# A value projection in seven block products instead of eight, on one Trainium2 core

## What is computed

```
xn = rms_norm(h, norm_in_g)
proj = einsum('btd,de->bte', xn, w_in)              # 1024 x 6144
q, k, v, g_ret, x_lru, g_lru = split(proj, 6)       # 1024 columns each
q = rotary(q); k = rotary(k) * 128 ** -0.5
scores = einsum(q, k) * decay_mat                   # 8 heads of 128, causal, decays by head
o_ret = group_norm_heads(scores @ v);  y_ret = o_ret * silu(g_ret)
xc = causal_depthwise_conv(x_lru)
o_lru = rg_lru(xc, gates);             y_lru = o_lru * silu(g_lru)
h = h + concat(y_ret, y_lru) @ w_out
```

## Time and profile before

| | |
|---|---|
| median of 3 runs | 2059.18 us (2058.5 to 2060.09) |
| the profiled execution: device time | 2056.59 us |
| its span | 2054.8 us |
| TensorE busy | 98% of the span |
| VectorE, GpSimd, ScalarE busy | 55%, 49%, 18% |
| mean granted TensorE clock | 0.996 |

### The profile page before, as it was taken

The page is one execution under the profiler, slowest core; times in us unless marked ns, Lnnn a source line. Parts: engine busy times, 40 slices in busy tenths (PEclk is TensorE's granted clock), DMA queues, the critical chain, the costliest instruction groups (busy, mean ns, idle before and its releaser), DMA issues.

```text
span 2054.8 us, 39352 instructions
## 1 busy us (share of the span) xinstructions
PE 2020.2 (98%) x16934; PEld 1900.2 (92%) x16934; DVE 1124.1 (55%) x1958; ACT 375.3 (18%) x777; POOL 1015.3 (49%) x775
## 2 busy tenths in 40 slices
PE   8999999999999999999899999999999999999998
PEld 7888887899998999978788999999999999999998
DVE  3535134456515675335757577726772455576752
ACT  1343012133201000024321210001000231120000
POOL 0000000258852788400001568885888677547884
PEclk9999999999999999999999999999999999999999
DMA  8634443344443454523102344444444544434441
GB/s 331 172 126 154 144 164 115 129 165 175 168 165 124 171 175 167 190 103 106 40 5 103 107 160 167 175 172 157 171 165 166 204 162 148 150 116 166 172 176 62
DMA packets 43878, 307.63 MB, mean 150 GB/s; under 512 B 5288, under 2 KB 5544, under 8 KB 7744
## 3 DMA queue, kind: packets, MB, share of 16 engines
q1 hardware_dynamic: 40752, 291.78, 39.9%
q0 software_dynamic: 2096, 7.31, 1.4%
q10 hardware_dynamic: 864, 6.10, 0.7%
HBM read 302.54 MB, written 2.62 MB: 149 GB/s over the span
## 4 chain that ended last, share of the span: by engine, by line
PE 91%; DVE 6%; issue 1%; ACT 1%; DMA 0%; DVEq 0%; SPq 0%
PE ps L587 57%; PE ps L252 15%; PE ps L311 5%; PE ps L249 3%; PE ps L271 1%; PE ps L286 1%; DVE sb_work L425 1%; PE ps L1658 1%; DVE sb_xn L2562 1%; DVE sb_work L418 1%; PE ps L1683 1%; PE ps L393 0%; DVE sb_h L788 0%; PE ps L2145 0%; PE ps L2292 0%
## 5 line engine op out<-in xcount | busy, mean ns | idle before, releaser
L587 PE MATMUL ps<-sb_work,sb_ring 128*128 128x128 f32 x3968 | 476.2, 275 | 0.3 <-DVE sb_work L1977 0.3
L587 PEld LDWEIGHTS ps<-sb_work,sb_ring 128*128 128x128 f32 x3968 | 459.4, 192 | 1.0 <-issue 0.5
L555 POOL TENSOR_TENSOR sb_table<-sb_ring 128x512 f32<-128x512 f32 x126 | 161.4, 1281 | 369.0 <-PE ps L587 189.8
L587 PE MATMUL ps<-sb_work,sb_table 128*128 128x128 f32 x2256 | 285.4, 275 | 0.0
L587 PEld LDWEIGHTS ps<-sb_work,sb_table 128*128 128x128 f32 x2256 | 268.4, 192 | 0.0
L558 POOL TENSOR_TENSOR sb_ring<-sb_ring 128x512 f32<-128x512 f32 x189 | 260.7, 1379 | 0.0
L557 POOL TENSOR_TENSOR sb_table<-sb_table,sb_ring 128x512 f32<-128x512 f32 x126 | 176.3, 1399 | 9.9
L587 PE MATMUL ps<-sb_xn,sb_ring 128*128 128x128 f32 x1440 | 175.5, 275 | 0.0
L587 PEld LDWEIGHTS ps<-sb_xn,sb_ring 128*128 128x128 f32 x1440 | 168.6, 192 | 0.4
L560 POOL TENSOR_TENSOR sb_table<-sb_ring,sb_table 128x512 f32<-128x512 f32 x126 | 168.4, 1336 | 0.0
L252 PE MATMUL ps<-sb_work,sb_ring 128*128 128x256 f32 x736 | 162.8, 380 | 0.0
(11 more groups left out here) (442 smaller groups left out, 2909.8 us busy)
## 6 DMA issues: line engine op xcount, KB each, us to landing
sb_ring<-stream SPq DMA_DIRECT2D x275, 1024.0 KB, 4.8
sb_table<-decay ACTq DMA_DIRECT2D x1, 1536.0 KB, 21.0
bias_rows<-sb_relg POOLq DMA_DIRECT2D x1, 1536.0 KB, 34.7
sb_con<-consts ACTq DMA_DIRECT2D x1, 1216.0 KB, 9.7
sb_table<-lora POOLq DMA_DIRECT2D x1, 1152.0 KB, 6.0
sb_h<-x SPq DMA_DIRECT2D x2, 512.0 KB, 5.8
sb_ring<-stream SPq DMA_DIRECT2D x2, 512.0 KB, 7.4
sb_work<-gates ACTq DMA_DIRECT2D x1, 1024.0 KB, 14.3
```

Source lines behind the costliest of these rows:

```text
L555: v.tensor_tensor(s[:, 0], a[1][0], a[1][1], ALU.add).then_inc(S["fw_ready"], 1)
L587: ins = mm(fast_bank(c, g, b)[:, i * P:i * P + P], *(sides[::-1] if token_major else sides), start=first and i == 0 and j == 0, stop=last ...
```

## The change

The v stage becomes four seven-product units. `plan()` now gives it no banks of the turn (the later stages keep the same bank numbers modulo four), and the stage comes first in the list of seven-product stages:

```diff
-("b1_v", 4, 0)
+("b1_v", 0, 4)
-FAST_ORDER = ["b2_ffn", "l0_ffn1", ...]
+FAST_ORDER = ["b1_v", "b2_ffn", "l0_ffn1", ...]
+def early_tile(c, z):
+    if z % PREPS:
+        flat = c.table[:, :, :].rearrange("p a b -> p (a b)")[:, 1536 * (z - 1):1536 * z]
+    else:
+        flat = c.work[4][:, :, :].rearrange("p a b -> p (a b)")[:, 0:1536]
+    return flat.rearrange("p (s k n) -> p s k n", s=3, k=4)
+def fast_base(g):
+    return 2 * (g % 2) + (0 if g < FAST_G["b2_ffn"] else 4)
```

TensorE:

```diff
 def lru_gates(n):
     if n == 0:
-        pe.wait_ge(S["decay_loaded"], 32)
+        pe.wait_ge(S["decay_loaded"], 16)
...
 for u in range(4):
-    p_unit(c, pe, n0 + u, q1 + u, c.xn, token_major=True)
+    pe.wait_ge(S["fw_ready"], 4 * u + 4)
+    if u < 2:
+        for q in (2 * u, 2 * u + 1):
+            c.wait_read(pe, PLAN["b1_k"][1] + q)
+    else:
+        pe.wait_ge(S["fast_read"], u - 1)
+    fast_products(c, pe, n0 + u, u, range(4), lambda k, j, t: c.xn[:, 2 * k + j, t * P:t * P + P],
+                  lambda k, m: xt[:, m, k, :], u, True, True,
+                  (lambda: pe.wait_ge(S["b1_spread"], 4)) if u == 0 else None, True)\
+        .then_inc(S[f"unit_done{(n0 + u) % UNITS}"], 1)
     lru_gates(u + 3)
...
 scores(0)
+pe.wait_ge(S["fast_read"], 3)
 gate_unit(0)
 gate_unit(1)
+pe.wait_ge(S["fast_read"], 4)
 outputs(0)
```

VectorE and ScalarE:

```diff
 for u in range(8):
     rotate(u)
     if u >= 5:
         decay(u - 5)
-for n in range(3, 8):
-    decay(n)
+spread_input(c, dve, c.xn, W[3], S["b1_spread"], 0)
+for u in range(4):
+    if u > 1:
+        dve.wait_ge(S["b1_v_kept"], u - 1)
+    fast_sum(c, dve, u, c.t1[:, u % 2, :], lambda: c.wait_done(dve, PLAN["b1_v"][0] + u), ch)
+    decay(u + 3)
+decay(7)
...
-dve.wait_ge(S["decay_loaded"], 32)
+dve.wait_ge(S["decay_loaded"], 48)
```

```diff
 for u in range(4):
-    c.wait_done(act, n0 + u)
-    c.read(nc.scalar.activation(v[:, :, u * 256:u * 256 + 256],
-                                c.bank(q0 + u).rearrange("p (m n) -> p m n", m=2), ACT.Copy), q0 + u)
+    copy_first(c, act, u)
+    if u > 1:
+        c.wait_done(act, PLAN["b1_v"][0] + u - 1)
+        act.dma_start(c.table[:, 4 * u - 8:4 * u - 4, :], c.decay[:, 4 * u - 8:4 * u - 4, :])\
+            .then_inc(S["decay_loaded"], 16)
+    act.wait_ge(S["fast_read"], u + 1)
+    nc.scalar.activation(v[:, :, u * 256:u * 256 + 256].rearrange("p t (i n) -> p i t n", i=2),
+                         c.t1[:, u % 2, :].rearrange("p (i t n) -> p i t n", i=2, t=2), ACT.Copy)\
+        .then_inc(S["b1_v_kept"], 1)
     lru_gates(u + 3)
...
 act.dma_start(c.gates[:, :, :, :], gates).then_inc(S["decay_loaded"], 16)
-act.dma_start(c.table[:, :, :], decay).then_inc(S["decay_loaded"], 16)
```

GpSimd prepares the four v units after the convolution (which is done with its inputs by then) and before it writes the bias rows:

```diff
+pool.wait_ge(S["b1_conv"], 8)
+prepare_weights(c, pool, "b1_v")

 pool.wait_ge(S["b2_bias_read"], 1)
 pool.dma_start(bias_rows...
```

More of the change, by code:

```diff
@@ L35, in plan @@
     fast = ("fast", 2, 3 * FFI - 2)
-    stages = [("b1_xlru", 4, 0), ("b1_q", 4, 0), ("b1_k", 4, 0), ("b1_v", 4, 0), ("b1_gret", 4, 0),
+    stages = [("b1_xlru", 4, 0), ("b1_q", 4, 0), ("b1_k", 4, 0), ("b1_v", 0, 4), ("b1_gret", 4, 0),
               ("b1_glru", 4, 0), ("b1_out", 0, 8),
@@ L493 @@
 FAST = ["b2_ffn", "l0_ffn1", "l0_ffn2", "l1_ffn1", "l1_ffn2"]
-FAST_ORDER = ["b2_ffn", "l0_ffn1", "l0_x", "l0_ffn2", "l1_ffn1", "gm", "l1_x", "l1_ffn2"]
+FAST_ORDER = ["b1_v", "b2_ffn", "l0_ffn1", "l0_x", "l0_ffn2", "l1_ffn1", "gm", "l1_x", "l1_ffn2"]
 PREPS = 3
@@ L502, in fast_counts @@
     for name in FAST_ORDER:
-        if name == "gm":
+        if name == "b1_v":
+            start, units, outs = PLAN[name][0], 4, 4
+        elif name == "gm":
             start, units, outs = PLAN["gm_v"][0], 22, 18
@@ L525, in x_count @@
     return spread_count(2 * i + 2) - 16
+def early_tile(c, z):
[4 more added lines that the diff above has]
+    return flat.rearrange("p (s k n) -> p s k n", s=3, k=4)
 def prep_tile(c, z):
-    tile = (z + 1) % PREPS
+    if z < FAST_Z["b2_ffn"]:
+        return early_tile(c, z)
+    tile = (z - FAST_Z["b2_ffn"] + 1) % PREPS
     if tile < 2:
@@ L560, in prepare_weights @@
         v.tensor_tensor(s[:, 2], a[0][1], s[:, 1], ALU.subtract).then_inc(S["fw_ready"], 1)
+def fast_base(g):
+    return 2 * (g % 2) + (0 if g < FAST_G["b2_ffn"] else 4)
 def fast_bank(c, g, b):
-    return c.ps[:, 4 + 2 * (g % 2) + b, :]
+    return c.ps[:, fast_base(g) + b, :]
 def fast_products(c, pe, n, z, pairs, xs, ts, g, first, last, before_t=None, token_major=False,
@@ L700, in fast_sum @@
     v, S = c.nc.vector, c.S
-    two = c.ps[:, 4 + 2 * (g % 2):6 + 2 * (g % 2), :].rearrange("p b n -> p (b n)")
+    two = c.ps[:, fast_base(g):fast_base(g) + 2, :].rearrange("p b n -> p (b n)")
     dve.wait_ge(S["fast_p1"], g + 1)
@@ L826, in b1_scalar @@
                                     c.bank(q0 + u).rearrange("p (m t) -> p m t", m=2), ACT.Copy), q0 + u)
-    act.wait_ge(S["b1_abs"], 1)
+    act.wait_ge(S["b1_pad"], 2)
     nc.scalar.activation(c.small[:, 8:16], c.small[:, 0:8], ACT.Exp, scale=-1.0).then_inc(S["b1_exp"], 1)
@@ L857, in b1_scalar @@
             lru_gates(u - 5)
-    n0, q0 = PLAN["b1_v"]
     v = W[2][:, :, :].rearrange("p a b -> p (a b)").rearrange("p (m n) -> p m n", m=2)
     for u in range(4):
-        c.wait_done(act, n0 + u)
-        c.read(nc.scalar.activation(v[:, :, u * 256:u * 256 + 256],
-                                    c.bank(q0 + u).rearrange("p (m n) -> p m n", m=2), ACT.Copy), q0 + u)
+        copy_first(c, act, u)
[7 more added lines that the diff above has]
+            .then_inc(S["b1_v_kept"], 1)
         lru_gates(u + 3)
@@ L924, in b1_tensor @@
             lru_gates(u - 5)
-    n0, q1 = PLAN["b1_v"]
+    n0, _ = PLAN["b1_v"]
+    xt = W[3][:, :, :].rearrange("p a b -> p (a b)").rearrange("p (s k t) -> p s k t", s=4, k=4)
     for u in range(4):
-        p_unit(c, pe, n0 + u, q1 + u, c.xn, token_major=True)
+        pe.wait_ge(S["fw_ready"], 4 * u + 4)
[8 more added lines that the diff above has]
+            .then_inc(S[f"unit_done{(n0 + u) % UNITS}"], 1)
         lru_gates(u + 3)
@@ L947, in outputs @@
             pe.wait_ge(S["b1_gate_i"], 8)
-            c.wait_read(pe, q1 + 3)
-            c.wait_read(pe, q1 + 2)
+            pe.wait_ge(S["b1_v_kept"], 4)
         else:
@@ L1016, in b1_vector @@
     ch.step(v.tensor_scalar(s[:, 16:24], c.p("lru_lambda", 0, 8), -1.0, None, ALU.mult))
-    v.tensor_tensor(s[:, 0:8], s[:, 16:24], c.p("lru_lambda", 0, 8), ALU.max).then_inc(S["b1_abs"], 1)
+    v.tensor_tensor(s[:, 0:8], s[:, 16:24], c.p("lru_lambda", 0, 8), ALU.max).then_inc(S["b1_pad"], 1)
     ch.step(v.tensor_scalar(s[:, 16:24], s[:, 16:24], 0.0, None, ALU.max))
@@ L1067, in decay @@
         dve.wait_ge(S["b1_gate_i"], n + 1)
-        v.scalar_tensor_tensor(out=W[5][:, n, :], in0=tmp[:, 1, :], scalar=1.0, in1=W[5][:, n, :],
-                               op0=ALU.add, op1=ALU.mult).then_inc(S["b1_ix"], 1)
+        ch.step(v.scalar_tensor_tensor(out=W[5][:, n, :], in0=tmp[:, 1, :], scalar=1.0, in1=W[5][:, n, :],
+                                       op0=ALU.add, op1=ALU.mult))
         dve.wait_ge(S["b1_gate_ready"], 4 * n + 4)
@@ L1117, in recurrence @@
             dve.wait_ge(S["b1_mult"], 1)
-            dve.wait_ge(S["b1_ix"], 8)
         for n in (2 * p, 2 * p + 1):
@@ L1211, in ln_vector @@
         else:
-            g, new = 2 * (FFI - 1) + b, c.t1[:, b % 2, :]
+            g, new = FAST_G["b2_ffn"] + 2 * (FFI - 1) + b, c.t1[:, b % 2, :]
             fast_sum(c, dve, g, new, lambda: wait_bank(c, dve, "b2_ffn", n, b), ch)
@@ L1509, in tap0 @@
             src = (c.t1, c.hid)[g][:, i % 2, :]
-            act.wait_ge(S["fast_read"], 2 * i - 1 + g)
+            act.wait_ge(S["fast_read"], FAST_G["b2_ffn"] + 2 * i - 1 + g)
             nc.scalar.activation(conv_bank(c, g), src, ACT.Copy).then_inc(S["b2_tap0"], 1)
@@ L1522, in conv_scalar @@
         if i:
-            copy_first(c, act, 2 * i - 2)
+            copy_first(c, act, FAST_G["b2_ffn"] + 2 * i - 2)
         tap0(i, 0)
@@ L1526, in conv_scalar @@
             keep(i - 1)
-            copy_first(c, act, 2 * i - 1)
+            copy_first(c, act, FAST_G["b2_ffn"] + 2 * i - 1)
         act.wait_ge(S["b2_tap"], 8 * i + 4)
@@ L1533, in conv_scalar @@
     for b in range(4):
-        copy_first(c, act, 2 * (FFI - 1) + b)
+        copy_first(c, act, FAST_G["b2_ffn"] + 2 * (FFI - 1) + b)
 def conv_vector(c, dve, V, ch):
@@ L1577, in conv_vector @@
         if i:
-            fast_sum(c, dve, 2 * i - 2, c.t1[:, i % 2, :], lambda: c.wait_done(dve, n0 + 2 * i), ch)
+            fast_sum(c, dve, FAST_G["b2_ffn"] + 2 * i - 2, c.t1[:, i % 2, :], lambda: c.wait_done(dve, n0 + 2 * i), ch)
             taps(i - 1, 1)
@@ L1582, in conv_vector @@
         if i:
-            fast_sum(c, dve, 2 * i - 1, c.hid[:, i % 2, :], lambda: c.wait_done(dve, n0 + 2 * i + 1), ch)
+            fast_sum(c, dve, FAST_G["b2_ffn"] + 2 * i - 1, c.hid[:, i % 2, :], lambda: c.wait_done(dve, n0 + 2 * i + 1),
+                     ch)
             spread_hidden(i - 1)
@@ L2789, in build @@
```

(2 more changed lines are left out.)

## The result

The changed kernel takes 2071.16 us, the median of 4 runs (2068.33 to 2073.41), against 2059.06 us before (4 runs, 2058.5 to 2060.09). The ratio is 1.0056 with a 95% interval of 1.0044 to 1.0069: slower by 12.1 us. The forecast was 2064.4 us with a range up to 2067.5: the sign was right, the size was less than half of it. The profiled execution took 2068.33 us, 11.7 more than the profiled one before.

The account below looks back on a forecast made before the run. TensorE, busy for 98% of the span, was taken as the bound. Saving -2.6, new wait +5.8 and half clock +2.0 gave +5.2 us on 2059.18: 2064.4 us, range 2061.0 to 2067.5.

Parts of the forecast that it names:

- The saving: Four v units on TensorE: each costs 6.26 instead of 6.91 us, saving 2.6 us.
- The new wait: First v unit, third product: TensorE waits from 98.9 to 104.7 us for VectorE's four combinations, 5.8 us late.
- The clock after it: Behind the pause at 99 us: TensorE's granted clock falls to half, costing 2.0 us, between nothing and 4.0.
- these three terms: First block's v units on TensorE: saving -2.6, new wait +5.8, half clock +2.0, together +5.2 us.
- Decay table ... I take under 10 us, nearer to the stream's row, as the stream is the main traffic beside the bias rows then: Table's second half, issued at 129.9 us: lands in under 10 us, before scores are wanted at 149.5.
- The term for the decay table: Scores times decays in the first block: the later table load costs TensorE nothing.
- The bounds, 4.2 and 21.0 us: Landing of the table's second half: 4.2 us from a scaled stream unit, 21.0 from the whole table in the opening.
- The rival: Decay table lands late, at 150.9 us; TensorE waits 2.4 us for the scores: 2066.8 us, chance 0.06.

Follow-up runs that it names:

- e1: The changed kernel with VectorE's four activation combinations behind decay(0) instead of behind decay(2): 2062.66 us, ratio 1.0016.
- e7: The kernel before, ordinary v units and early decay table, plus four unread combinations behind decay(2) and TensorE's wait for them: 2065.78 us, ratio 1.0037.
- e6: e3 with 12 unused matmuls of 128 x 256 put on TensorE ahead of its wait for the combinations: 2062.58 us, ratio 1.0011.
- e3: The changed kernel with the decay table loaded in the opening and weight sums of v units 1 and 3 in the convolution's buffer: 2065.10 us, ratio 1.0024.
- e5: The changed kernel with GpSimd writing the bias rows only after both halves of the decay table have landed: 2065.80 us, ratio 1.0029.
- e2: The changed kernel with GpSimd issuing the bias rows' write before the v units' weight sums, not behind them: 2069.22 us, ratio 1.0040.
- e8: The changed kernel with the combinations behind decay(0) and the bias rows written after the decay table has landed: 2057.51 us, ratio 0.9994.
- e10: e8 run once more on another chip: 2055.51 us, ratio 0.9988.

## Why the prediction was wrong

**The saving: right.** 6.26 us a unit, 2.61 us in all, in every version.

**The new wait: right.** Forecast 5.8 us, measured 5.80, at the place and with the releaser named. e1 shows that moving four VectorE instructions removes it, e7 that they alone bring it.

**The clock after it: right, its size in part by luck.** Forecast 2.0 us from the earlier trace rows, measured 1.64 here, 1.54 by the difference of e6 and e3, 1.84 in e7, and 2.74 in e5 (40 records in 112.47 - 105.26 = 7.21 us). All lie within the bounds of 0 and 4.0. That 2.0 came so near was in part luck, as the price hangs on when in the pause the clock falls. Together these three terms were to give +5.2, and e3, which has them alone, measured +4.84 in the stretch and a median 5.0 us above before.

**"Decay table ... I take under 10 us, nearer to the stream's row, as the stream is the main traffic beside the bias rows then": this step failed.** The second half took 22.0 us. The term for the decay table stood at nothing in the sum and measured 3.43 us of wait and 1.69 us of half clock, together 5.12 us. The bounds, 4.2 and 21.0 us, were drawn nearly right, and the upper one was the case; the choice between them was wrong. I took the stream's 5.6 us from the earlier trace rows, a median over 200 us of which most have no other traffic, and read the bias rows' line only for its own landing time. The trace before held a row that warns. DMA issues from 61 to 100 us, while the bias rows (34.7 us) were written:

```profile
sb_ring<-stream SPq DMA_DIRECT2D x5, 1024.0 KB, 18.1
```

A stream unit takes 18.1 us there, more than three times the 5.6, and the two issued between 66 and 80 us take 24.0 and 22.8. The sum had room for a landing of 149.5 - 1.0 - 129.9 = 18.6 us. Scaled to 768 KB as the prediction did, 18.1 and 24.0 us become 13.6 and 18.0, still just in time. So this row does not give the wait; it shows that "under 10 us" does not hold beside the write and that the margin was nearly gone, so a chance of 0.06 was too small. The scaling by size failed too: the second half, 768 KB, took 22.0 us, and the 1 MB unit issued between 125 and 132 us took 24.9, of which three quarters are 18.7. The move of the bias rows from 62 to 117 us, which the prediction noted, put their write onto the table's load; e2 puts it back and e5 behind, and in both the halves land in about 4.1 us.

The Trainium skill, "DMA: Bandwidth & Descriptors", section "Queues, rings and completion order", says that each DMA engine takes the queues that have work in turn, a packet at a time. The trace agrees in that SP's and ScalarE's transfers both slow down beside GpSimd's write (21.1 us, and 11.6 and 22.0 us).

Why this write weighs so much more than its 1.5 MB is not shown by any run, but the traces say where it shows. From 140 to 143 us in e5 it has the DMA engines to itself (queue, packets, MB, share of the 16 engines' time):

```profile
q0 software_dynamic: 32, 0.15, 46.2%
```

Alone it keeps a little under half of the engines' time and moves 49 GB/s, where other traffic reaches 426 (e5, 100 to 101 us). The table's own packets are not slower beside it: they take 12.2% of the 37 us from 116 to 153 us, 4.5 us, and 27.9% of 18 us, 5.0 us, in e5 without it (118 to 136 us). So the load waits between its packets. That would fit a write carried by half of the engines only, which holds up every load that needs all of them. No run changes the write's shape, so this stays an argument.

**The rival's price was too low as well.** I gave it 2.4 us for the wait. It measured 3.43, as the landing took 1.0 us more than the upper bound of 21.0. And I forgot that this wait, too, idles TensorE: the clock fell a second time, another 1.69 us. The same cost had been put into the sum for the first wait.

**What stays open.** The changed kernel's median lies 12.1 us above before, the stretch explains 9.95, the opening 0.4. The 1.4 us in later blocks need no cause in the change: what follows the stretch takes 1852.1 to 1857.2 us in the twelve profiles, 1853.2 before and 1854.5 in the changed kernel, and e8 and e10, one and the same kernel on two chips, differ there by 3.8 us. Part of it is the clock at the stage of the earlier trace rows: it was low from 865.0 to 871.8 us before and from 872.9 to 883.1 us in the changed kernel. There it fell while TensorE was shown busy in every slice of 1 us from 860 to 873 us, so idle time is not the only thing that comes before a fall; no run tells what else does.

**Where the expected gain went.** The four units by themselves are a gain of 2.6 us. It was turned into a loss by two things beside TensorE: four VectorE instructions behind work that they don't need, and a DMA issue that moved because a preparation was put ahead of it in GpSimd's queue.

## What to carry over

When a step moves on one queue, everything behind it in that queue moves too: look up what a moved DMA will run beside, and read landing times from a window in which that neighbour was active, not from a median over the whole stage. Where a consumer needs inputs that have long been there, put their making into the last idle time of its engine before the need, not behind the work of the moment. And add to every new wait of TensorE the half clock behind it: pauses of 3.3 to 8.5 us here cost 1.6 to 3.0 us more than their length.

## What was unexpected of the hardware

- The write of the bias rows (1.5 MB from 8 partitions, each read 128 times over, 1024 rows of 1.5 KB; issued by GpSimd) took 34.4 to 35.8 us wherever it ran, and a 1 MB load beside it 15.5 to 21.2 us (medians) instead of about 5, a 768 KB load 11.6 and 22.0 us instead of 4.1 to 4.5.
- A wait of 3.3 us on TensorE already brought the clock to 0.50, at 152.7 us, about when the matmuls resumed: the price was paid wholly behind the wait.
- After pauses of 5.64 to 5.65 us the granted clock was low for 6.8 us in all four profiles (the changed kernel, e3, e5, e7). What differed is when it fell: 2.1 to 2.4 us into the pause in three, 4.4 in e5. The part behind the restart was 3.3 to 3.5 us, and 5.6 in e5, and cost half of its length. So the same pause has no fixed price. Twenty-four records without use, in place of the idle time, kept the clock at 1.00.
- Beside GpSimd's weight sums in e2, all five instructions of `decay(1)` slowed down, the TENSOR_SCALAR with a single input tensor from 0.29 to 1.24 us as well; the first instruction of `rotate(7)`, which reads PSUM, kept its 0.68 us.
